# Two more experts with fixed places in a two-layer mixture-of-experts kernel, and the ends of both layers reordered

## The reference

```python
def hier_moe(h, w_rg, b_rg, w_re, b_re, w_g, w_u, w_d):
    ...
    ids = g_idx * E_PER_GROUP + top_i                      # two experts of one group per token
    gates = jnp.sum(jax.nn.one_hot(ids, N_EXPERTS) * wts[..., None], axis=1)
    hid = jax.nn.silu(jnp.einsum("nd,edf->nef", x, w_g)) * jnp.einsum("nd,edf->nef", x, w_u)
    y = jnp.einsum("nef,efd->nd", hid * gates[:, :, None], w_d)

x = x + g2 * hier_moe(h, ...)        # at the end of each layer
return rms_norm(x, final_norm)       # after layer 1
```

## Time and profile before

| | us |
|---|---|
| median of 3 runs | 843.94 (842.47 to 844.89) |
| the profiled execution | 846.4 |
| its span, first to last instruction | 844.6 |
| TensorE busy | 789.3 (93%) |
| VectorE, ScalarE busy | 321.8, 166.8 |
| DMA queue of SP, share of 16 DMA engines | 86.5% |
| granted TensorE clock, mean | 0.973 |

### The profile page before, as it was taken

How to read it: one execution, slowest core, us unless ns; L and a number is a source line. 1 busy time by engine, 2 the same in 40 slices (tenths; PEclk the granted TensorE clock), 3 DMA queues, 4 the chain that set the end, 5 groups by cost and what they waited for, 6 DMA issues and landing times.

```text
span 844.6 us, 15977 instructions
## 1 busy us (share of the span) xinstructions
PE 789.3 (93%) x6913; PEld 525.5 (62%) x6913; DVE 321.8 (38%) x687; ACT 166.8 (20%) x323; POOL 12.3 (1%) x17
## 2 busy tenths in 40 slices
PE   3999999998999999999986989989999999999787
PEld 3788568677798665456542444779865555644335
DVE  1155467653414433433332340241543443333224
ACT  3112411323203111111110141130311111111012
POOL 0000001020000000000000000000000000000000
PEclk9999999999999999999998999999999999999898
DMA  9999779493899299999999999996549999999991
GB/s 342 387 371 386 260 261 349 147 345 108 270 393 395 111 417 410 402 416 415 420 414 412 401 386 385 388 409 269 199 168 416 407 398 417 415 421 416 410 398 70
DMA packets 97879, 291.47 MB, mean 345 GB/s; under 512 B 11833, under 2 KB 14991, under 8 KB 87567
## 3 DMA queue, kind: packets, MB, share of 16 engines
q1 hardware_dynamic: 86960, 284.32, 86.5%
q10 hardware_dynamic: 10847, 6.11, 2.5%
HBM read 288.30 MB, written 2.10 MB: 344 GB/s over the span
## 4 chain that ended last, share of the span: by engine, by line
PE 70%; SPq 11%; DMA 11%; ACT 3%; DVE 3%; issue 2%; ACTq 1%; DVEq 0%
PE psum L1357 7%; PE psum L1264 7%; PE psum L907 7%; PE psum L1343 5%; PE psum L1333 5%; PE psum L967 5%; DMA ring<-in_w_exp_up 5%; DMA scratch<-in_w_exp_up 5%; PE psum L860 5%; SPq L744 5%; PE psum L1389 4%; PE psum L1515 3%; PE psum L1528 3%; PE psum L1400 3%; SPq L733 2%
## 5 line engine op out<-in xcount | busy, mean ns | idle before, releaser
L1343 PE MATMUL psum<-scratch,hT 128*32 128x512 f32 (+1 forms) x384 | 79.5, 659 | 15.1 <-DMA ring<-in_w_exp_up 8.6
L1333 PE MATMUL psum<-scratch 128*128 128x128 f32 x704 | 84.0, 279 | 0.9 <-DVE scratch L2460 0.9
L1333 PEld LDWEIGHTS psum<-scratch 128*128 128x128 f32 x704 | 82.0, 195 | 1.2 <-issue 1.2
L1343 PE MATMUL psum<-ring,hT 128*32 128x512 f32 (+1 forms) x288 | 69.9, 641 | 2.5 <-DMA scratch<-in_w_exp_up 2.5
L907 PE MATMUL psum<-hT,ring 128*128 128x256 f32 x256 | 57.8, 382 | 1.1 <-DVE hT L2051 0.7
L1400 PEld LDWEIGHTS psum<-const,scratch 128*128 128x128 bf16 x480 | 45.1, 97 | 21.5 <-issue 13.6
L1400 PE MATMUL psum<-const,scratch 128*128 128x256 bf16 x480 | 55.9, 272 | 1.5 <-DVE scratch L2476 1.5
L2469 DVE TENSOR_SCALAR hT<-psum,const 128x512 f32<-128x512 f32 x22 | 16.5, 751 | 106.3 <-PE psum L1389 93.6
L1343 PEld LDWEIGHTS psum<-scratch,hT 128*32 128x32 f32 (+1 forms) x384 | 21.4, 123 | 54.5 <-issue 54.5
L907 PEld LDWEIGHTS psum<-hT,ring 128*128 128x128 f32 x256 | 47.8, 190 | 9.6 <-DVE hT L2051 2.0
L1885 ACT ACTIVATE scratch<-psum 128x256 f32<-128x256 f32 x22 | 8.5, 384 | 210.0 <-PE psum L1343 123.2
(11 more groups left out here) (334 smaller groups left out, 1032.8 us busy)
## 6 DMA issues: line engine op xcount, KB each, us to landing
ring<-in_w_mod SPq DMA_DIRECT2D x40, 1024.0 KB, 11.4
scratch<-in_w_exp_down SPq DMA_DIRECT2D x28, 1024.0 KB, 16.2
ring<-in_w_exp_down SPq DMA_DIRECT2D x24, 1024.0 KB, 17.4
scratch<-in_w_exp_gate SPq DMA_DIRECT2D x22, 1024.0 KB, 16.8
scratch<-in_w_exp_up SPq DMA_DIRECT2D x22, 1024.0 KB, 18.4
ring<-in_w_exp_gate SPq DMA_DIRECT2D x18, 1024.0 KB, 15.5
ring<-in_w_exp_up SPq DMA_DIRECT2D x18, 1024.0 KB, 18.2
scratch<-in_w_exp_gate SPq DMA_DIRECT2D x26, 512.0 KB, 11.0
```

The source lines that it names most:

```text
L1333: last = mm(bank[b][:, k * P:(k + 1) * P], hrow[:, t, half * 4 + k, :], Pm[:, t, :], start=(t == 0), stop=(t == 1))
L1343: last = mm(bank[0][i * m:(i + 1) * m, :], xg[:, k, i * m:(i + 1) * m], w[e][:, k, :, :], start=(k == 0), stop=(k == KT - 1))
```

## The change

Experts 6 and 7 get fixed places of 32 rows each, so 24 experts are ordered instead of 26. The fourth pass is a three of experts 6, 7 and rank 3 (64 rows); the ninth ordered quad takes the place of the old three, tenth in the row. Counts of passes, slots and matmuls of experts stay. SP's wait for `v_pos` moves from the pass's start to its first "r" entry. In `moe_further`, on the branch that is taken here, VectorE adds quarter 0 before `weighted_rows`, and does the final products of quarters 0 and 1 together, and of 2 and 3 together; TensorE loads and branches before `scatter_last(1)`, and in layer 1 sums the squares of quarter 0 there in place of the idle products. The other sums are spread between the transposes.

```diff
-NFIX = 6
+NFIX = 8
+NPAIR = 3
...
-          ("quad", [("r", 6 + i) for i in range(4)], 24), ("pair", [("r", 1), ("r", 2)], 16),
-          ("quad", [("r", 10 + i) for i in range(4)], 28), ("mono", [("r", 0)], 12),
-          ("quad", [("r", 14 + i) for i in range(4)], 32), ("quad", [("r", 18 + i) for i in range(4)], 36),
-          ("three", [("r", 3), ("r", 4), ("r", 5)], 20), ("quad", [("r", 22 + i) for i in range(4)], 40)]
+          ("three", [("e", 6), ("e", 7), ("r", 3)], 20), ("quad", [("r", 4 + i) for i in range(4)], 24),
+          ("pair", [("r", 1), ("r", 2)], 16), ("quad", [("r", 8 + i) for i in range(4)], 28), ("mono", [("r", 0)], 12),
+          ("quad", [("r", 12 + i) for i in range(4)], 32), ("quad", [("r", 16 + i) for i in range(4)], 36),
+          ("quad", [("r", 20 + i) for i in range(4)], 40)]
...
-SHARE = {"mono": [0], "pair": [0, 1], "three": [0, 0, 1, 2], "quad": [0, 1, 2, 3]}
+SHARE = {"mono": [0], "pair": [0, 1], "three": [0, 1, 2, 2], "quad": [0, 1, 2, 3]}
...
                     c = moe_at[l] + PASS_AT[q]
-                    if q == NFIX // 2:
-                        sp.wait_ge(S.v_pos, 3 * l + 3)
                     ids = []
                     for kind, e in PASSES[q][1]:
                         if kind == "r":
+                            if q == NPAIR:
+                                sp.wait_ge(S.v_pos, 3 * l + 3)
                             e = sp.value_load(route_i[0:1, l, 9 + e:10 + e], min_val=0, max_val=NE - 1)
                         ids.append(e)
...
                         last_down(c + nu, 1).then_inc(S.used, nd)
-                        idle_products(3, 3)
-                        pe.wait_ge(S.m_yr1, n + 1)
-                        scatter_last(1).then_inc(S.t_fin, 1)
...
+            def square_sums(b):
+
+                pe.wait_ge(S.a_sq, SQ0[5] + b + 1)
+                for k in (2 * b, 2 * b + 1):
+                    for t in range(NB):
+                        last = mm(bank[t][:, 0:1], sqm[:, k, t * P:(t + 1) * P], ones[:, 0:1],
+                                  start=(k == 0), stop=(k == KT - 1), skip_group_check=True)
+                return last
...
                 with pe.Else():
-                    pe.nop()
+                    if l == DEPTH - 1:
+                        square_sums(0)
+                    else:
+                        idle_products(3, 3)
+                    pe.wait_ge(S.m_yr1, (l + 1) * NPASS)
+                    scatter_last(1).then_inc(S.t_fin, 1)
...
+            square_sums(1)
             rows_out(0)
-            for k in range(KT):
...
-            last.then_inc(S.t_ms, 1)
+            square_sums(2)
+            square_sums(3).then_inc(S.t_ms, 1)
             rows_out(1)
...
                 with dve.Else():
-                    dve.nop()
-
-                for b in range(4):
-                    dve.wait_ge(S.t_fin, 2 * l + 1 + b // 2)
-                    add_scaled(bank[4 + b], b, l * MT + 5 * KT).then_inc(S.v_y, 1)
+                    add_experts(l, 0)
+                    dve.wait_ge(S.used, done)
+                    weighted_rows().then_inc(S.m_yr1, 1)
+                    add_experts(l, 1)
                     if l == DEPTH - 1:
...
+                        final_weights(0)
+                        final_weights(1)
+                    add_experts(l, 2)
+                    add_experts(l, 3)
+                    if l == DEPTH - 1:
+                        final_weights(2)
+                        final_weights(3)
```

More of the change, by code:

```diff
@@ L439, in build @@
         vtk = part(2048, (NB, D))
-        sqo = part(4096, (KT, T))
         vsq = part(6144, (D,))
@@ L503, in build @@
         yrow = part(12000, (NB, D))
-        sqf = part(14100, (KT, T))
+        finl = part(2304, (4, NB, P))
         ab = small[:, 0:32]
@@ L1557, in rows_out @@
                     for k in range(4):
-                        last = nc.tensor.transpose(bank[2 + 2 * t + half][:, k * P:(k + 1) * P], hT[:, half * 4 + k, t, :], ident)
+                        last = nc.tensor.transpose(bank[2 + 2 * t + half][:, k * P:(k + 1) * P],
+                                                   finl[:, k, t, :] if half == 0 else hT[:, 4 + k, t, :], ident)
                     last.then_inc(S.t_last, 1)
+            square_sums(1)
             rows_out(0)
-            for k in range(KT):
-                if k % 2 == 0:
-                    pe.wait_ge(S.a_sq, SQ0[5] + k // 2 + 1)
-                for t in range(NB):
-                    last = mm(bank[t][:, 0:1], sqf[:, k, t * P:(t + 1) * P], ones[:, 0:1],
-                              start=(k == 0), stop=(k == KT - 1), skip_group_check=True)
-            last.then_inc(S.t_ms, 1)
+            square_sums(2)
+            square_sums(3).then_inc(S.t_ms, 1)
             rows_out(1)
@@ L2572, in moe_experts, with add_experts, final_weights @@
                         split(3).then_inc(S.m_yr1, 1)
-                    else:
-                        weighted_rows().then_inc(S.m_yr1, 1)
                     if q == 2:
                         further_tables(l)
+            def add_experts(l, b):
+                dve.wait_ge(S.t_fin, 2 * l + 1 + b // 2)
+                add_scaled(bank[4 + b], b, l * MT + 5 * KT).then_inc(S.v_y, 1)
+            def final_weights(b):
+                dve.wait_ge(S.v_y, 4 * (DEPTH - 1) + b + 1)
+                for k in (2 * b, 2 * b + 1):
+                    dst = finl[:, k, :, :] if b < 2 else hT[:, k, :, :]
+                    last = V.tensor_scalar(dst.rearrange("p t n -> p (t n)"), xT[:, k, :, :].rearrange("p t n -> p (t n)"),
+                                           cols[:, V_FIN + k:V_FIN + k + 1], None, ALU.mult)
+                if b % 2 == 1:
+                    last.then_inc(S.v_last, 1)
             def moe_further(l):
                 f = FS[l]
+                done = moe_at[l] + MOE_SLOTS
                 n = dve.value_load(route_i[0:1, l, 0:1], min_val=0, max_val=OVF // 2)
                 with dve.If(n > 0):
+                    dve.wait_ge(S.used, done)
+                    weighted_rows().then_inc(S.m_yr1, 1)
                     dve.wait_ge(S.m_gat, 2 * (l + 1) * NPASS)
```

30 lines of the change are left out of this document (18 added, 12 removed).

## The result

| | before | changed |
|---|---|---|
| median, us | 844.41 (842.47 to 846.39, 8 runs) | **852.92** (850.36 to 857.31, 8 runs) |
| the profiled execution, its span | 846.4, 844.6 | 851.99, 850.0 |

The ratio is 1.0101, with a 95% interval of 1.008 to 1.0123: the change makes the kernel 8.5 us slower. The forecast had the direction (848.2, +4.3) but half of the size, and its range ended at 851.0.

The account below looks back on a forecast made before the run. Up to a dip in the DMA rate at the fourth pass TensorE's pace bounds each layer, behind it the weight stream. Passes +5.1, clock +2.0, ends -2.7 and -0.1 give +4.3 on 843.94: 848.2 us, range 843.8 to 851.0.

Parts of the forecast that it names:

- Regimes, dip and reset: Each layer: TensorE sets the pace until SP's queue runs dry at the fourth pass, then the weight stream; earlier leads vanish there.
- The rival in which the early restart goes through: Slot window does not set the stream, so each layer gains the 2.0 us of register loads: 837.1 us, chance 0.05.
- Register loads, 0: Three register loads move behind the pass's DMAs; the stream restarts 2.0 us earlier per layer, costed at nothing.
- The three in fourth place, +2.5 per layer: Half-filled slot in the 11-slot window at the dip leaves 1.05 MB more behind it: +2.5 us per layer, bounds 0 and 3.3.
- The clock, +1.0 per layer: Last pass: longer gap before the second half of gate and up lowers TensorE's clock, 0 to 1.8 us, taken as +1.0 per layer.
- The ends, -2.7 and -0.1: Layer ends: earlier quarter 0 add, paired final products and spread sums give -2.7 us in layer 1, -0.1 in layer 0.
- Load and branch, 0: TensorE's load and branch ahead of scatter_last(1) are covered by 1.9 us of last_down(1): cost nothing.
- The rival in which the branch stalls TensorE: Stall for instruction fetch ahead of scatter_last(1), up to 1 us per layer more than forecast: 850.2 us, chance 0.05.
- Sum: Whole kernel: +5.1 passes, +2.0 clock, -2.7 and -0.1 ends make +4.3 us on the median of 843.94.
- all three cases that made it: Forecast 848.2 us (0.65), late stream without clock fall 846.2 (0.2), branch stall 850.2 (0.05); together 843.8 to 851.0.

Follow-up runs that it names:

- loads put back: Changed kernel with three more register loads between SP's wait for the expert order and its first DMA: 853.38 us, ratio 1.0091.
- 6 and 7 ahead of the order: Changed kernel, but SP issues the gate and up loads of experts 6 and 7 before its wait for the expert order: 854.04 us, ratio 1.0113.
- the filled slot: Changed kernel, but the three's odd down matrix is loaded a second time into the empty half of its slot: 853.36 us, ratio 1.0087.
- quads behind the dip: Changed kernel with the pair of ranks 1 and 2 moved behind both quads (three, quad, quad, pair, mono): 848.68 us, ratio 1.0031.
- short rows: The quads behind the dip kernel, with positions 20 to 22 filled by four 0.52 MB loads each in rows of 4 KB: 851.11 us, ratio 1.0072.
- the new passes alone: Kernel before with the new table of passes and SP's wait at the first ordered expert, old ends kept: 857.08 us, ratio 1.0134.
- the cut by partitions: The quads behind the dip kernel, with positions 20 to 22 filled by four 0.52 MB loads each over 64 partitions, rows of 8 KB: 876.89 us, ratio 1.0391.
- fourth pass by halves: New ends with the old passes, the fourth pass (a quad) taking its gate and up weights by halves: 845.89 us, ratio 0.9991.
- idle products: Changed kernel with seven more idle products in the last pass, between the scatter and the second half of gate and up: 856.34 us, ratio 1.0138.
- the ends alone: Changed kernel with the old table of passes and six fixed experts, so only the new ends remain: 843.32 us, ratio 0.9973.
- early halves: New ends; fourth pass a quad of experts 6, 7 and ranks 6, 7 by halves, its first slot issued before the order: 842.02 us, ratio 0.9959.

## Why the prediction was right in direction and short in size

- **Regimes, dip and reset**: right in kind. Byte curves that start 0.5 MB (loads put back) or 2.64 MB (6 and 7 ahead of the order) apart meet again. But they meet 38 us behind the first product, at the smaller hole behind the second pass, not at the dip 20 us later. The rival in which the early restart goes through is ruled out. By this the rule to issue early and wait late (the Trainium skill, "DMA: Bandwidth & Descriptors", section "Rules for kernel authors") has no effect ahead of such a reset.
- **Register loads, 0**: right, 1.0091 with them and 1.0101 without; 4 us more would have been 1.0148.
- **The three in fourth place, +2.5 per layer**: this step failed, and by size. Its first part, the half slot of 1.05 MB, holds (the filled slot; the deficit of 1.10 to 1.15 MB with quads behind the dip). What it missed is the restart. The step took position 20 as a load like any other. With a three of five slots ahead of a quad of six, position 20 is the pair's first, by halves; before, it was a quad's. These loads cost another 0.7 MB, 1.7 us per layer (with the passes held the same, short rows cost 0.8 MB in layer 0 and 0.4 in layer 1). The upper bound was 3.3, "with 0.4 us per layer for a slower restart of an emptier queue". No row is named for the 0.4, and 2.5 + 0.4 is 2.9, not 3.3. The only restart that the rows of before show at the dip is one of large loads; a bound has to come from the same form of load. The term measures +4.5 per layer (1.84 MB at 413 GB/s; the mean of +5.3 and +3.8), 9.0 in all in place of 5.1.
- **The clock, +1.0 per layer**: right in kind and near in size, the latter partly by luck. In the changed kernel, the new passes alone, the filled slot, the loads put back and 6 and 7 ahead of the order, the profiles show the fall in 8 of 10 last passes. It costs 1.5 to 1.7 us in seven of them and 2.9 in one, 1.4 per layer. The reason given for 1.0, that part of the fall is wasted in the gap, does not hold: in those seven the half clock begins within 0.4 us of the first product and costs its full price. The old passes show no fall in 6. The gap's length alone does not decide: 3.09 and twice 3.12 us (the second in the cut by partitions, layer 1) were without a fall, other gaps of 3.12 with one; 1.71 us (fourth pass by halves, layer 0) without, 1.45 with idle products ahead of it with one.
- **The ends, -2.7 and -0.1**: right, a little smaller: 2.3 us less in all by the ratio of the ends alone, and 2.3 from the end of last_down(1) to the last sum in layer 1.
- **Load and branch, 0**: right; 0.03 us between last_down(1) and the sums in layer 1, and no gap in layer 0. The rival in which the branch stalls TensorE is ruled out in this profile.
- **Sum**: +9.0 + 2.8 - 2.3 - 0.1 = +9.4 against a measured +8.5 (6.8 to 10.4 by the interval). The range ended at 851.0 because all three cases that made it had the same 5.1 for the passes; the term's own upper bound was never carried to the range's end. With it, 0.8 us more per layer, the end would have been 852.6, still just short.

## What to carry to other kernels

In a stream through a window of slots, count the bytes inside the window at the point where it closes, not the bytes of the whole: a half-filled slot there is lost bandwidth, and one behind it costs nothing. Then look at which transfers stand first behind the point, and in which form; large transfers (here 1.05 MB) belong there, small ones where the queue is deep. What is gained ahead of such a point (an earlier restart, earlier loads) is worth nothing until the point itself moves.

## What the hardware showed that was not expected

- Loads of 0.52 MB in rows of 4 KB run at full rate in a deep queue (0.16 us a packet; 420 GB/s at 348 to 350 in the changed kernel), but into an emptied one at 240 to 352 GB/s in stretches of 4 to 8 us, with the engines' share at 0.81 and more. This was seen at the dip (changed kernel, filled slot, short rows) and, at 335 GB/s, at the order (fourth pass by halves). Most packets are as short as ever; a minority (139 of 1084 at the dip of the changed kernel) take up to 1.4 us. The changed kernel in layer 0 has a pause of 2 us in the middle of its slow stretch; why it is slow again behind it is open.
- Loads of 1.05 MB are back at their rate some 2 to 3 us behind a restart, in rows of 8 KB (401 to 424 GB/s at the dip and at the order) and in rows of 4 KB (down matrices, 345 to 416 GB/s from 2 to 5 us behind the issue, in both layers of eight profiles). The version with early halves, whose queue ran dry twice within 4 us, took 4 us (373, then 414 GB/s).
- Loads over 64 of 128 partitions, the two halves one behind the other, run at 222 GB/s in place of 409.
- The stream holds 413 to 415 GB/s over 120 us and more. The Trainium skill, "DMA: Bandwidth & Descriptors", section "Where 436 GB/s comes from", has some 358 GB/s as what HBM gives one core and names a measured transfer of 16 MB at 425 GB/s beside it; here the measurement decides, and it is near the second.
